# Two-layer decoder step on one core: retention's first loads, its sample state updates and the recurrence's output products are moved

## The reference

```python
# layer 0, recurrence: 4 heads, 128 x 128 state
o_inter = einsum('bhtk,bhkv->bhtv', qc * exp(bcum), S)
o_intra = einsum('bhts,bhsv->bhtv', scores, vc)
S_new = exp(blast)[..., None] * S + einsum('bhsk,bhsv->bhkv', kc * exp(blast - bcum), vc)
# layer 1, retention: 4 heads, 256 x 512 state, chunks of 128 tokens
o_inter = einsum('bhtk,bhkv->bhtv', qc, S) * q_decay
o_intra = einsum('bhts,bhsv->bhtv', einsum('bhtk,bhsk->bhts', qc, kc) * intra_decay, vc)
S_new = chunk_decay * S + einsum('bhsk,bhsv->bhkv', kc * k_decay, vc)
y = x + (rms_norm(o) * silu(g)) @ w_out
```

## Time and profile before

| | us |
|---|---|
| median of 3 runs | 2111.87 |
| lowest and highest | 2105.89, 2114.35 |
| profiled execution, its own time | 2108.48 |
| its span in the trace | 2106.7 |
| recurrence's last head ends, about | 966 |
| odd projection's last matmul starts | 1671.45 |
| retention's first matmul starts | 1676.88 |

### The profile page before, as it was taken

How to read it: one execution, slowest core, us unless ns; L and a number is a source line. 1 busy time by engine, 2 the same in 40 slices (tenths; PEclk the granted TensorE clock), 3 DMA queues, 4 the chain that set the end, 5 groups by cost and what they waited for, 6 DMA issues and landing times. The chain is left out here.

```text
span 2106.7 us, 31304 instructions
## 1 busy us (share of the span) xinstructions
PE 1906.9 (91%) x11538; PEld 1531.5 (73%) x11538; DVE 857.6 (41%) x1480; ACT 522.5 (25%) x1133; POOL 594.5 (28%) x532
## 2 busy tenths in 40 slices
PE   6999999968887787586999999999999879999998
PEld 6788998954444454475889999888788747777776
DVE  3551000047787455664435443111000055656564
ACT  5210110135565433242430000000111132323231
POOL 3332222025655301513034232222222052212120
PEclk9999999968888898597999999999999989999999
DMA  4232222051243264615433333222224287655643
GB/s 149 90 113 95 93 104 93 34 175 55 75 130 100 61 198 147 206 56 184 140 124 93 105 93 103 88 87 87 83 88 140 72 262 211 211 179 179 202 137 125
DMA packets 210238, 261.57 MB, mean 124 GB/s; under 512 B 24260, under 2 KB 150916, under 8 KB 209860
## 3 DMA queue, kind: packets, MB, share of 16 engines
q1 hardware_dynamic: 154436, 199.53, 30.5%
q10 hardware_dynamic: 53680, 55.14, 8.0%
q0 software_dynamic: 2000, 5.25, 0.8%
HBM read 176.10 MB, written 81.40 MB: 122 GB/s over the span
## 5 line engine op out<-in xcount | busy, mean ns | idle before, releaser
L415 PE MATMUL odd_bank<-odd_w_hi,odd_h_hi 128*128 128x512 f32 x576 | 224.8, 390 | 2.5 <-DVE odd_shared L767 2.5
L415 PE MATMUL odd_bank<-odd_w_lo,odd_h_hi 128*128 128x512 f32 x576 | 224.8, 390 | 0.0
L415 PE MATMUL odd_bank<-odd_w_hi,odd_h_lo 128*128 128x512 f32 x512 | 199.7, 390 | 0.0
L363 POOL CAST odd_w_hi<-odd_raw 128x1024 fp32r<-128x1024 f32 x48 | 51.5, 1073 | 338.0 <-PE odd_bank L415 313.7
L415 PE MATMUL even_bank<-even_h_hi,even_w_hi 128*128 128x362 f32 (+1 forms) x384 | 127.0, 331 | 4.5 <-DVE even_stage_tm L767 4.5
L415 PE MATMUL odd_bank<-odd_h_hi,odd_w_hi 128*128 128x362 f32 (+1 forms) x384 | 126.0, 328 | 1.8 <-POOL odd_w_lo L365 1.8
L415 PEld LDWEIGHTS odd_bank<-odd_w_hi,odd_h_hi 128*128 128x128 f32 x576 | 108.5, 188 | 25.5 <-DVE odd_shared L767 2.9
L415 PE MATMUL even_bank<-even_h_hi,even_w_lo 128*128 128x362 f32 (+1 forms) x384 | 126.6, 330 | 0.0
L415 PE MATMUL even_bank<-even_h_lo,even_w_hi 128*128 128x362 f32 (+1 forms) x384 | 126.4, 329 | 0.0
L415 PE MATMUL odd_bank<-odd_h_lo,odd_w_hi 128*128 128x362 f32 (+1 forms) x384 | 126.0, 328 | 0.0
L415 PE MATMUL odd_bank<-odd_h_hi,odd_w_lo 128*128 128x362 f32 (+1 forms) x384 | 125.0, 326 | 0.0
(11 more groups left out here) (331 smaller groups left out, 4123.9 us busy)
## 6 DMA issues: line engine op xcount, KB each, us to landing
odd_raw<-in_w_in_odd SPq DMA_DIRECT2D x48, 512.0 KB, 3.9
even_raw<-in_w_in_even SPq DMA_DIRECT2D x32, 512.0 KB, 3.8
k_page<-in_cache_k SPq DMA_DIRECT2D x64, 256.0 KB, 3.1
v_page<-in_cache_v SPq DMA_DIRECT2D x64, 256.0 KB, 3.1
out_ret_sample<-rt_s SPq DMA_DIRECT2D x32, 512.0 KB, 3.3
ahead_place<-in_state_ret SPq DMA_DIRECT2D x24, 512.0 KB, 5.6
v_tm<-odd_shared ACTq DMA_DIRECT2D x64, 128.0 KB, 2.0
g_tm<-odd_shared ACTq DMA_DIRECT2D x64, 128.0 KB, 2.0
```

What stands on the lines that cost most here:

```text
L363: nc.gpsimd.tensor_copy(hi, r).then_inc(w_hi_done, 1)
L415: mm = pe.matmul(out, stationary, moving, start=(j == 0), stop=(j == len(pairs) - 1))
```

## The change

Five edits. (1) `Ahead` loads the samples' q, k and v and the first two tiles of the output weights instead of three samples' states; it waits in addition until the projection's weights are all split (`w_split`). The weights go to a tensor `ahead.raw` that the odd projection uses for its own raw weights, and that later holds y tiles 3 and 4. (2) SP's list in retention begins with s0 of sample 0 and gets s0 1 to 3 by and by; the later s0 are loaded 2, 1 and 1 in the steps 2, 3 and 0 of a group of four, instead of 3 and 1 in the steps 2 and 3. (3) The state update of sample c is made one step later on PE, DVE and SP (`sample_states(n - 1)` in step n, the last behind the loop). (4) At the start ACT and DVE split the samples' values first, then the keys; ACT's `prepare(1)` goes ahead of the first stacking DMAs. (5) In the recurrence PE's output products are made in two halves, chunks 0 to 3 in portion 4 behind a wait for four states, 4 to 7 in portion 5; ACT squares each half in the same portion.

```diff
     def load(self, sp):
@@ ahead
-            sp.dma_start(s0[n], state_in[n, 0].rearrange("(j k) v -> k j v", k=P)).then_inc(self.s0_in[n], 16)
+            if n == 0:
+                for dst, src in zip(self.samples(s1), (q_fm, k_fm)):
+                    sp.dma_start(dst, by_head(src)[1].rearrange("h p j t -> p h j t")).then_inc(self.smp_qk, 16)
+                sp.dma_start(v_s, v_tm[TP:T].rearrange("t (h n) -> t h n", n=DV)).then_inc(self.smp_v, 16)
         sp.dma_start(flat(q_dec), tables[:, 5 * P:9 * P]).then_inc(self.q_dec_in, 16)
+        for r in range(2):
+            sp.dma_start(self.raw[:, r, :], weight[r * P:r * P + P, :]).then_inc(self.raw_in[r], 16)
@@ project_in_now
+                sp.wait_ge(w_split, 2 * NBLK)
                 ahead.load(sp)
@@ hgrn_now, ACT
                 yield
                 yield
-                yield
                 squares(h, 0)
+                yield
                 squares(h, 1)
@@ hgrn_now, PE
                 yield
-                yield
                 pe.wait_ge(q_moved, nth_move[h, NM - 1] + 1)
...
-                pe.wait_ge(state_done, NCH * (h + 1))
                 for c in range(NCH):
+                    if c % 4 == 0:
+                        pe.wait_ge(state_done, NCH * h + c + 4)
...
                     if c % 4 == 3:
                         mm.then_inc(o_done, 1)
-                yield
+                        yield
@@ retention_out, SP
-            for dst, src in ((q_s, q_cols_s), (k_s, k_cols_s)):
-                sp.dma_start(dst, src.rearrange("h p j t -> p h j t")).then_inc(smp_qk, 16)
-            sp.dma_start(v_s[:], v_rows[TP:T]).then_inc(smp_v, 16)
+            load_s0(0)
             load_g(0)
-            load_g(1)
             for x in ahead.left_tm:
                 sp.wait_ge(x, LEFT)
             load_raw(0)
+            load_g(1)
+            load_s0(1)
...
                         load_g(2)
+                        load_s0(2)
+                        load_s0(3)
                         load_y(0)
                         load_gs(0, 0)
-                        load_s0(3)
...
-                sp.wait_ge(s1_done, J * (n + 1))
-                sp.dma_start(state_samples[c, h].rearrange("(j k) v -> k j v", k=P), s1[n % 2][:]).then_inc(s1_left[n % 2], 16)
-                if n % SEQS >= 2 and n + 2 < NSTEP:
-                    sp.wait_ge(o_done, unit_of["samples", n // SEQS] + 1)
-                    for x in (n + 2, n + 3, n + 4) if n % SEQS == 2 else (n + 4,):
-                        load_s0(x)
+                if n:
+                    store_samples(n - 1)
+                    if (n - 1) % SEQS and n + 3 < NSTEP:
+                        sp.wait_ge(o_done, unit_of["samples", (n - 1) // SEQS] + 1)
+                        for x in (n + 2, n + 3) if (n - 1) % SEQS == 1 else (n + 3,):
+                            load_s0(x)
...
+            store_samples(NSTEP - 1)
             for h, t in outs[-NT:]:
@@ retention_out, PE
+            def sample_states(m):
+                h, c = divmod(m, NCH)
+                if m < NCH:
+                    pe.wait_ge(stacked[m], NSTACK)
+                    pe.wait_ge(stacked_k[m], NSTACK)
+                grp, rows = c // SEQS, slice(c % SEQS * ROWS, c % SEQS * ROWS + 3 * LS)
+                for j in range(J):
+                    pe.wait_ge(state_done, J * min(m + 1, NSTEP - 1) + j + 1)
+                    if m == NSTEP - 1:
+                        pe.wait_ge(s1_done, J * (m - 1) + j + 1)
+                    pe.matmul(u[j][:], k_stack[rows, grp, h, j], v_stack[rows, grp, h], start=True, stop=True,
+                              tile_position=(c % SEQS * ROWS, 0)).then_inc(us_done, 1)
...
                 for j in range(J):
-                    if n:
-                        pe.wait_ge(s1_done, J * (n - 1) + j + 1)
+                    if n >= 2:
+                        pe.wait_ge(s1_done, J * (n - 2) + j + 1)
...
-                if n < NCH:
-                    pe.wait_ge(stacked[n], NSTACK)
-                    pe.wait_ge(stacked_k[n], NSTACK)
-                grp, rows = c // SEQS, slice(c % SEQS * ROWS, c % SEQS * ROWS + 3 * LS)
-                for j in range(J):
-                    pe.wait_ge(state_done, J * n + j + 1)
-                    pe.matmul(u[j][:], k_stack[rows, grp, h, j], v_stack[rows, grp, h], start=True, stop=True,
-                              tile_position=(c % SEQS * ROWS, 0)).then_inc(us_done, 1)
+                if n:
+                    sample_states(n - 1)
                 for x in outs_in(n):
                     product_out(*x)
...
+            sample_states(NSTEP - 1)
@@ retention_out, ACT
             prepare(0)
+            act.wait_ge(smp_v, 16)
+            nc.scalar.copy(vs_hi, v_s).then_inc(first_vs_hi, 1)
             act.wait_ge(table_s_in, 16)
             for h in range(HC):
...
-            act.wait_ge(smp_v, 16)
-            nc.scalar.copy(vs_hi, v_s[:]).then_inc(first_vs_hi, 1)
+            prepare(1)
             act.wait_ge(first_vs_hi, 1)
             act.wait_ge(first_vs, 1)
             stack(0)
-            prepare(1)
@@ retention_out, DVE
             prepare(0)
+            dve.wait_ge(first_vs_hi, 1)
+            dve.tensor_tensor(vs_lo, v_s, vs_hi.bitcast(F32), ALU.subtract).then_inc(first_vs, 1)
             dve.wait_ge(table_s_in, 16)
...
-            dve.wait_ge(first_vs_hi, 1)
-            dve.tensor_tensor(vs_lo, v_s[:], vs_hi.bitcast(F32), ALU.subtract).then_inc(first_vs, 1)
             prepare(1)
...
+                if n:
+                    sample_states(n - 1)
...
+            sample_states(NSTEP - 1)
```

More of the change, by code:

```diff
@@ L107, with __init__ @@
 class Ahead:
-    N, NQ, NV, NS0 = 4 * T + 2 * T + 2 * D, 3, 3, 3
-    def __init__(self, nc, ctx, q_fm, k_fm, v_tm, state_in, tables):
+    N, NQ, NV = 4 * T + 2 * T + 2 * D, 3, 3
+    def __init__(self, nc, ctx, q_fm, k_fm, v_tm, tables, weight):
         sem = lambda n: nc.alloc_semaphore(f"ahead_{n}")
@@ L117, in __init__ @@
         self.k_dec = ctx.enter_context(nc.sbuf_tensor("ahead_k_dec", [P, HC], F32))
+        self.raw = ctx.enter_context(nc.sbuf_tensor("ahead_raw", [P, 2, D], F32))
         self.table_in, self.q_dec_in = sem("table_in"), sem("q_dec_in")
         self.qk_in, self.v_in = [sem(f"qk_in{i}") for i in range(self.NQ)], [sem(f"v_in{i}") for i in range(self.NV)]
-        self.s0_in = [sem(f"s0_in{i}") for i in range(NS // 2)]
+        self.smp_qk, self.smp_v, self.raw_in = sem("smp_qk"), sem("smp_v"), [sem(f"raw_in{r}") for r in range(DV // P)]
         self.left_tm = [sem(f"left_tm{i}") for i in range(NSTAGE)]
-        self.of = q_fm, k_fm, v_tm, state_in, tables
+        self.of = q_fm, k_fm, v_tm, tables, weight
     def at(self, first, n):
@@ L141, in in_retention @@
         ident, scm = self.at(6400, P), self.at(4096, 2 * P).rearrange("p (i n) -> p i n", i=2)
-        s0 = [self.at(first, 2 * DV).rearrange("p (j v) -> p j v", v=DV) for first in (4352, 5376, 7552)]
+        v_s = self.place[0:TS, 4352:6400].rearrange("t (h v) -> t h v", h=HC)
+        s1 = self.at(7552, 2 * DV).rearrange("p (j v) -> p j v", v=DV)
         qd = self.at(6528, 512).rearrange("p (i j t) -> p i j t", i=2, t=P)
         qd_s = self.at(7040, 512).rearrange("p (h j t) -> p h j t", h=HC, t=TS)
-        return q, k, v, decay, q_dec, ident, scm, s0, qd, qd_s
+        return q, k, v, decay, q_dec, ident, scm, v_s, s1, qd, qd_s
     def load(self, sp):
-        q_fm, k_fm, v_tm, state_in, tables = self.of
-        q, k, v, decay, q_dec, ident, _, s0, _, _ = self.in_retention()
+        q_fm, k_fm, v_tm, tables, weight = self.of
+        q, k, v, decay, q_dec, ident, _, v_s, s1, _, _ = self.in_retention()
         flat = lambda x: x.rearrange("p a b -> p (a b)")
@@ L198, in project_in_now @@
         eps = sb("eps", [P, 1])
-        raw = sb("raw", [P, 2, KD // 2, WBLK])
+        raw = sb("raw", [P, 2, KD // 2, WBLK]) if even else ahead.raw[:].rearrange("p s (c n) -> p s c n", n=WBLK)
         w_hi = sb("w_hi", [P, NSLOT, KD, WBLK], F32R)
@@ L1797, in rest @@
                 yield
+                squares(h, 0)
                 yield
-                squares(h, 0)
                 squares(h, 1)
@@ L2010, in project_out @@
         return
-    q_fm, k_fm, v_tm, _, state_in, _, _, _, consts = args = _held.pop("retention")
+    q_fm, k_fm, v_tm, *_, consts = args = _held.pop("retention")
     with nc.cleanup_on_exit(), ExitStack() as ctx:
-        ahead = Ahead(nc, ctx, q_fm, k_fm, v_tm, state_in, consts["ret_p"])
+        ahead = Ahead(nc, ctx, q_fm, k_fm, v_tm, consts["ret_p"], weight)
         project_in_now(nc, "odd", ahead, *_held.pop("odd"))
@@ L2052, in retention_out @@
         k_dec_s = table_s[:, HC * TS + NS:]
-        q, k, v, decay, q_dec, ident, scm, s0, qd, qd_s = ahead.in_retention()
+        q, k, v, decay, q_dec, ident, scm, v_s, s1_odd, qd, qd_s = ahead.in_retention()
         q_dec_s, k_dec = sb("q_dec_s", [P, HC, TS]), ahead.k_dec
@@ L2063, in retention_out @@
```

(30 more changed lines are left out.)

41 lines of the change are left out of this document (17 added, 24 removed).

## The result

The changed kernel takes 2097.95 us in the median of 15 runs (2089.42 to 2111.08); the kernel before took 2111.64 beside it (15 runs, 2105.88 to 2120.17). The ratio is 0.9941, 95% interval 0.9923 to 0.9958: 12.4 us less, 9 to 16. Run again beside the experiments it gave 2101.81 us (12 runs) and 0.9966 (0.9948 to 0.9985). So it is faster, by 7 us in one set of runs and 12 in the other. 2097.95 us lies inside my range of 2088 to 2103; I had forecast 17 us less. The profiled execution spans 2094.4 us (before 2106.7).

What follows compares the result with a forecast made beforehand. PE was taken as full from 1722 us on, leaving gains in retention's start and in PE's idle before the recurrence's output products. 9.4 + 7.7 = 17.1 us off gave 2094.5 us, range 2088 to 2103.

Steps and rivals of the forecast that it cites:

- rival (b): Retention's start: step 2's 2.69 us take 5.4 at 1.2 GHz, so retention gives 5.0 us; 2097.2 us; chance 0.14.
- Recurrence, 9.4 us forecast: Output products in halves cut PE's idle before them over four heads: 9.4 us, bounds 6.6 to 10.5.
- Heads 0 and 1: Recurrence: head 0's output products end 4.5 us earlier, 2.6 of it clock; head 1 gains 3.3.
- Heads 2 and 3: Recurrence: the halves gain 1.1 us in head 2 and 0.5 in head 3.
- Retention's start, 7.7 us forecast: Step 2's update starts 7.7 us earlier through edits 1 to 4; bounds 5 to 9.5.
- the samples off the path: Retention's start: all four loads of the samples leave the path, landing in the odd projection's last 80 us.
- POOL's weight subtractions as the next thing late: Retention's start: POOL's two weight subtractions (5.75 us) hold step 2, which starts 5.9 us earlier, at about 1705.1.
- 15.5 and 28.0 us: Sign: step 1 starts some 15 us, step 2 some 28 us behind retention's first matmul (34.2 before).
- from there PE is full: Retention: from step 2's update, 7.7 us ahead of 1715.51, PE works without gaps.
- (a): Retention's start gives nothing back, as a transfer still sets step 2; 9.4 us remain, 2102.5 us; chance 0.09.
- (c): Retention: later loads of s0 stall PE 10 us at each of three heads' starts; slower, 2124 us; chance 0.03.
- (d): Recurrence: a level behind a waiting half costs each head its gain; 7.7 us remain, 2104 us; chance 0.06.

Runs made afterwards that it cites:

- e_recurrence: The kernel before with edit 5 alone (the recurrence's output products in halves); 2101.41 us against 2109.53, ratio 0.9958.
- e_retention: The changed kernel with edit 5 undone (edits 1 to 4 alone); 2112.32 us against 2109.53, ratio 1.0011.
- e_best: The changed kernel with y's second tile and the samples' gates loaded later, and POOL's, DVE's and ACT's parts of the weight splitting moved later; 2095.21 us, 0.9927.
- e_filled: e_best with three more matmuls that nobody needs, on PE in front of step 1; 2090.77 us, ratio 0.9919.
- e_retention_loads: The changed kernel without edit 5, with y's second tile and the samples' gates loaded later; 2103.66 us against 2111.72, ratio 0.9968.
- e_late_k: The changed kernel with q and k of step 4 issued behind the values and gate of their round; 2101.01 us, ratio 0.995.

## Why the forecast was right, and where it was not

**The time.** 2097.95 us lies 3.4 above the forecast and within 1 us of rival (b), TensorE's clock, to which I gave 0.14. In the trace that case is what happened in retention: step 2 at 1.2 GHz, though at 4.05 us instead of 2.69, not 5.4. That the median falls so near it is in part luck: the second set gave 7 us instead of 12, and of the sum's two terms the timed runs bear out only the recurrence's (8.9 us alone), not retention's (nothing alone).

**Recurrence, 9.4 us forecast.** Heads 0 and 1 were right. Counted from the recurrence's first matmul, e_recurrence ends head 0's products 5.1 us earlier (0.9 of it from ahead of them: DVE's fourth state is there at 49.4 us instead of 50.4) and head 1's another 3.2; I had 4.5 and 3.3. Heads 2 and 3 were mis-sized: together -0.1 us instead of 1.6. In head 2 DVE's seven states start 14.4 us behind the end of head 1's products (927.87 in e_recurrence), where they started 13.4 behind it before: DVE's part of a head does not move up with PE's, so the first half begins only 0.6 us before the whole did (15.7 us behind the same place instead of 16.3). Over all traces the recurrence takes 143.0 us without edit 5 (four) and 135.8 with it (ten), 7.2 less; 1.3 of that is given back in the projection. There every trace has the same wait of 1.77 us for POOL, and behind it the clock fell in seven of 14, all of them with edit 5 (seven of ten; none of four without it); whether the edit or chance did that stays open. The timed gain of edit 5 alone, 8.9, is the forecast's size.

**Retention's start, 7.7 us forecast.** The steps up to step 2's start held to a few tenths: the samples off the path (three loads, not the four that I wrote), POOL's weight subtractions as the next thing late, 15.5 and 28.0 us. The step that failed is "from there PE is full". I costed the moves in SP's queue only for s0, and not for q and k of step 4. They are wanted 5.6 us sooner (34.5 us behind the first matmul instead of 40.1). They are issued 12.8 us sooner too, but into a full queue, behind s0, y and the gates: k takes 16.5 us to land instead of 4.4 and comes 1.0 late. That fewer bytes were queued in all, as I argued against (a), did not help the load that stood behind them. And I kept rival (b) second because one idle stretch of 1.79 us had left the clock alone. One row was no evidence: behind 2.07 us at the same place it fell in e_recurrence, behind 1.77 us in the projection in seven of 14 traces, behind 1.25 us in one of ten; and behind 2.3 us, ahead of step 0's update in e_retention, e_best and e_filled, it did not. The Trainium skill, "TensorE: Matmul & The Clock Gate", "What's actually happening", which I cited for (b), says that idleness closes the gate. These traces agree in so far as the low level comes behind idle stretches, and where I set one row against the rule I was wrong to; but stretches of equal length at the same place went either way.

**The parts do not add.** Edits 1 to 4 gave 0.0 and +0.1% alone; against edit 5 alone (0.9958) the changed kernel was 4 us better in its first set of runs (0.9941) and 2 us worse in its second (0.9966). That the late k and the clock behind it can eat the gain is shown in one of the four traces with the early start and the early loads (44.6 us against 40.4, 40.6 and 41.1); the time of e_retention_loads fits it. How often it happens in unprofiled executions stays open, and e_late_k's unchanged time speaks against putting all of it there. So why edits 1 to 4 alone, 3.7 and 4.2 us ahead in their two traces, gain nothing in 24 timed executions is not shown.

**The others.** (a), a transfer holding step 2, did not happen; a transfer held step 4. (c): no wait of PE for s0 in the trace. (d): the level between the halves held nothing back.

## What to carry over

When a change lets an engine start earlier, list every buffer that it will want earlier in the next two rounds, and look where their loads stand in the queue: 128 KB took 16.5 us to land behind a full queue, 8.0 when 1 MB of loads was moved from ahead of it (later edits with the same order still saw up to 15.8), and 4.4 in the kernel before. Count the waits that a change leaves, not only their sum: one wait of 10.6 us followed by full-rate work was worth as much as four short ones that began step 1 8 us sooner. Where executions of one kernel differ by 20 us, a single trace shows one draw; cut several at the same places before a loss is put down to an edit.

## What was not expected of the hardware

Idle of the same length at the same place, 1.25 us ahead of head 2's first products, was followed by 1.2 GHz in one trace of the changed kernel and by 2.4 in the other; 1.77 us ahead of the same projection matmul went seven times each way in 14 traces. What it costs is mostly not the wait but what comes behind: 4.2 us in all for a wait 0.9 us longer, in the one pair of traces that shows it. Three idle-time matmuls (2.74 us of work nobody needs) kept the level up and brought step 1's end forward by 2.2 us, against a level that was low in all ten traces without them. And within each kernel 0.001 of mean granted clock went with 1.55 us of time.
